# Own places for a stage's first four tiles, last rows put off, and a final norm with tokens on partitions, in a three-layer fp32 network on one core

## What is computed

```python
for i in range(2):
    h = rmsnorm(hres, norm_g[i, 0])
    m = diff_attention(h, ...) if i == 0 else short_conv(h, w_in, conv_w, w_out)
    hres = hres + rmsnorm(m, norm_g[i, 1])
    h = rmsnorm(hres, norm_g[i, 2])
    hres = hres + rmsnorm(square(relu(h @ w_up[i])) @ w_down[i], norm_g[i, 3])
x = hres[:, 16:]
# short_conv: b, c, u = split(h @ w_in); u = c * u; y = causal 3-tap conv(u); out = (b * y) @ w_out
h = rmsnorm(x, norm_gain)
z = h @ w_in                     # 25 tiles of 128 features: pool input, gates, r, k, v, decay, a
y_a = pool(...); y_b = rwkv7_time_mix(token_shift(...), ...)
x = x + concat(y_a * silu(g_a), y_b * silu(g_b)) @ w_out
out = rmsnorm(x, final_gain)
```

## Time and profile before

| | |
|---|---|
| three runs, us | 1639.82, 1643.88, 1643.98 |
| median, us | 1643.88 |
| the profiled execution: its own time / span, us | 1643.31 / 1641.5 |
| mean granted TensorE clock | 0.981 |
| TensorE products busy | 1564.2 us |
| VectorE / ScalarE / GpSimd busy | 786.0 / 619.6 / 525.7 us |

### The profile page before, as it was taken

The page is one execution under the profiler, slowest core; times in us unless marked ns, Lnnn a source line. Parts: engine busy times, 40 slices in busy tenths (PEclk is TensorE's granted clock), DMA queues, the critical chain, the costliest instruction groups (busy, mean ns, idle before and its releaser), DMA issues.

```text
span 1641.5 us, 31463 instructions
## 1 busy us (share of the span) xinstructions
PE 1564.2 (95%) x12704; PEld 1394.3 (85%) x12704; DVE 786.0 (48%) x1374; ACT 619.6 (38%) x1139; POOL 525.7 (32%) x233
## 2 busy tenths in 40 slices
PE   8999998999999999999999999999999889999895
PEld 7898978989999999989989788888889767778764
DVE  5434443754132331664436642322316798656645
ACT  5666664543132232432224532322224534433321
POOL 2222222044444444134430444444440244540020
PEclk9999999999999999999999999999999999999998
DMA  5111211132222232222222232232322122200001
GB/s 196 53 52 53 65 53 64 53 103 91 90 91 92 96 96 91 78 73 89 95 77 78 78 102 90 92 101 90 96 96 78 52 90 85 82 16 3 3 27 51
DMA packets 35691, 125.69 MB, mean 77 GB/s; under 512 B 4080, under 2 KB 4336, under 8 KB 35568
## 3 DMA queue, kind: packets, MB, share of 16 engines
q1 hardware_dynamic: 35568, 123.90, 23.5%
HBM read 121.79 MB, written 2.10 MB: 75 GB/s over the span
## 4 chain that ended last, share of the span: by engine, by line
PE 70%; DVE 11%; issue 3%; ACT 2%; DVEq 0%; ACTq 0%
PE G L1461 58%; PE ST L1782 3%; PE G L1782 3%; PE PV L1782 1%; PE PO L1782 1%; DVE wlo L922 1%; DVE rstd L883 1%; DVE m L942 1%; PE ST L1427 1%; DVE hres L949 1%; DVE acc L1351 0%; DVE t L1201 0%; DVE z L1204 0%; PE PO L1461 0%; DVE z L1193 0%
## 5 line engine op out<-in xcount | busy, mean ns | idle before, releaser
L465 POOL TENSOR_TENSOR wlo<-raw,whi 128x1024 fp32r<-128x1024 f32 x207 | 502.5, 2428 | 1073.1 <-ACT whi L517 636.7
L1461 PE MATMUL G<-xh,whi 128*128 128x258 f32 (+3 forms) x1504 | 369.6, 308 | 15.9 <-DVE t L1028 5.4
L1461 PE MATMUL G<-xl,whi 128*128 128x258 f32 (+3 forms) x1504 | 359.7, 302 | 0.0
L1461 PE MATMUL G<-xh,wlo 128*128 128x258 f32 (+3 forms) x1504 | 357.8, 300 | 1.1 <-DVE xl L890 1.1
L1461 PE MATMUL G<-ah,whi 128*128 128x256 f32 (+2 forms) x1024 | 279.6, 314 | 4.7 <-DVE al L1176 2.9
L1461 PEld LDWEIGHTS G<-xh,whi 128*128 128x128 f32 x1504 | 244.4, 190 | 39.7 <-issue 17.3
L1461 PE MATMUL G<-ah,wlo 128*128 128x256 f32 (+2 forms) x1024 | 277.8, 312 | 0.0
L1461 PE MATMUL G<-al,whi 128*128 128x256 f32 (+2 forms) x1024 | 277.7, 312 | 0.0
L527 ACT ACTIVATE whi<-raw 128x1024 fp32r<-128x1024 f32 x112 | 118.8, 1060 | 415.5 <-PE G L1461 407.4
L1461 PEld LDWEIGHTS G<-xh,wlo 128*128 128x128 f32 x1504 | 245.8, 190 | 11.0 <-DVE xl L890 1.4
L1461 PEld LDWEIGHTS G<-xl,whi 128*128 128x128 f32 x1504 | 245.1, 190 | 9.9
(11 more groups left out here) (322 smaller groups left out, 1991.3 us busy)
## 6 DMA issues: line engine op xcount, KB each, us to landing
raw<-weights_dram SPq DMA_DIRECT2D x225, 512.0 KB, 3.5
hres<-xT_dram SPq DMA_DIRECT2D x8, 264.0 KB, 5.1
out_dram<-hres SPq DMA_DIRECT2D x8, 256.0 KB, 2.1
con<-consts_dram SPq DMA_DIRECT2D x1, 512.0 KB, 7.2
mat<-mats_dram SPq DMA_DIRECT2D x1, 512.0 KB, 8.0
con<-consts_dram SPq DMA_DIRECT2D x1, 264.0 KB, 6.6
vec<-vecs_dram SPq DMA_DIRECT2D x1, 171.0 KB, 6.4
con<-consts_dram SPq DMA_DIRECT2D x1, 128.0 KB, 4.0
```

Of the source, the lines that this page charges most:

```text
L465: nc.gpsimd.tensor_tensor(wlo[:, s], raw[:, s % 2], whi[:, s].bitcast(F32), ALU.subtract)\
L1461: last_of[0] = nc.tensor.matmul(to[:, p0:p1], wt[:, w, ws], xt[:, k, t0 - off:t1_ - off], start=k == 0 and q == 0, stop=k == KT - 1 and q ...
```

## The change

**Own places, four tiles in a row.** In the first MLP chunk tiles 0 to 3 are taken out in a row, tiles 2 and 3 into the two `sq` buffers, before any low part. ScalarE reads them there. In the convolution tiles 0 to 3 are taken out before row 0 is worked on; rows use in turn `cb` and a set made of `t1` and `sq`. In the input stage tiles 0 to 3 are taken out first, and later tiles use banks 0 to 3 in turn, so that a tile waits for the fourth tile before it and not for the second.

**Late rows put off.** In the convolution's output product tile 0 and tile 1 take steps 0 to 6, then both take step 7. In the last output product seven rows are open instead of six: the seven parts of row 6 come before the parts with k = 7.

**Last norm.** TensorE multiplies chunks of 128 tokens of the squares with one column of ones, so that sums have tokens on partitions, 128x4. Root and reciprocal are of 128x4. Eight products of the broadcast reciprocal with the identity, four for each of banks 1 and 2, spread it over partitions again. VectorE scales rows 0, 1, 2, 3, 6, 7 with bank 1 as operand. ScalarE has scaled rows 4 and 5 by their gain ahead of time, copies bank 2 to `t1`, and GpSimd multiplies rows 4 and 5. Rows are stored in the order 0, 1, 2, 4, 3, 6, 5, 7.

```diff
-O2_TILES = [(o, k) for o in range(OPEN) for k in range(KT - 1)] + [(o, KT - 1) for o in range(OPEN)]
-O2_TILES += [(o, k) for o in range(OPEN, KT) for k in range(KT)]
+O2_TILES = [(o, k) for o in range(OPEN + 1) for k in range(KT - 1)] + [(o, KT - 1) for o in range(OPEN + 1)]
+O2_TILES += [(KT - 1, k) for k in range(KT)]
...
+BESIDE, ALONE = (4, 5), (0, 1, 2, 3, 6, 7)
+LAST_ORDER = (0, 1, 2, 4, 3, 6, 5, 7)
...
+        def squared_tile(c, j, s4):
+
+            return sq[:, s4 % 2] if c == 0 and j in (2, 3) else t1[:, s4 % 2]
...
+            pool.wait_ge(S("rstd_copied"), len(BESIDE) + 1)
+            for k in BESIDE:
+                nc.gpsimd.tensor_tensor(hres[:, k, META:], hres[:, k, META:], t1[:, 0, 0:SEQ], ALU.mult)\
+                    .then_inc(S("beside_ready"), 1)
...
-            stat_root(9, OUT)
+                if j - 1 in BESIDE:
+                    nc.scalar.activation(hres[:, j - 1, META:], hres[:, j - 1, META:], ACT.Copy, scale=col(V_FG, j - 1))\
+                        .then_inc(S("rstd_copied"), 1)
+            act.wait_ge(post_sum, 9)
+            nc.scalar.activation(rms[:, 0:4], G[0][:, 0:4], ACT.Sqrt, scale=1.0 / D, bias=eps_t[:, 0:1]).then_inc(rms_ready, 1)
+            act.wait_ge(S("rstd_spread"), 2)
+            nc.scalar.activation(t1[:, 0, 0:SEQ], G[1][:, 0:BANK], ACT.Copy).then_inc(S("rstd_copied"), 1)
...
-                            if n0 or c or not isinstance(j, int) or j >= 2:
+                            if c or j >= 4:
                                 dve.wait_ge(sqr_ready, j + (n0 - 1))
...
                         if c == 0:
                             for j in range(8):
-                                if j != 1:
-                                    evict(b0 + UP[c] + j, j, (b0 + UP[c] + j) % 4)
                                 if j == 0:
-                                    evict(b0 + UP[c] + 1, 1, (b0 + UP[c] + 1) % 4)
-                                low(j, (b0 + UP[c] + j) % 4)
+                                    for n in range(HELD):
+                                        evict(b0 + UP[c] + n, n, n)
+                                elif j >= HELD:
+                                    evict(b0 + UP[c] + j, j, j % 4)
+                                low(j, j % 4)
...
+            def conv_tiles(j):
+
+                return [cb[:, r] for r in range(3)] if j % 2 == 0 else [t1[:, 0, 0:NW], t1[:, 1, 0:NW], sq[:, 0, 0:NW]]
...
+            for n in range(HELD):
+                conv_tile(n)
             for j in range(KT):
...
+                for n in range(max(HELD, 3 * j), 3 * j + 3):
+                    conv_tile(n)
...
+            for j in range(HELD):
+                input_tile(j)
+            for j in range(25):
+                b = B_IN2 + j
+                if j >= HELD:
+                    input_tile(j)
...
-            stat_recip(9, OUT)
-            dve.wait_ge(rstd_ready, stat_count(9))
-            for k in range(KT):
-                nc.vector.scalar_tensor_tensor(hres[:, k, META:], hres[:, k, META:], col(V_FG, k), rstd[:, 1, META:], ALU.mult,
+            dve.wait_ge(rms_ready, stat_count(9))
+            nc.vector.reciprocal(rstd[:, 1, 0:4], rms[:, 0:4]).then_inc(rstd_ready, 1)
+            dve.wait_ge(S("rstd_spread"), 1)
+            for k in ALONE:
+                nc.vector.scalar_tensor_tensor(hres[:, k, META:], hres[:, k, META:], col(V_FG, k), G[0][:, BANK:], ALU.mult,
                                                ALU.mult).then_inc(S("out_ready"), 1)
...
-            product(B_CO, 8, a_ready, 40, ah[1], al[1], OUT, OUT[0], end=2)
+            for ks in (range(KT - 1), [KT - 1]):
+                for j in range(2):
+                    if ks[0] == 0:
+                        begin(B_CO + j)
+                    for k in ks:
+                        pe.wait_ge(a_ready, 40 + k + 1)
+                        some(G[j], j, [k], ah[1], al[1], OUT[0], block_part(OUT))
+                    if ks[0]:
+                        last_of[0].then_inc(block_done, 1)
+            product(B_CO, 8, a_ready, 40, ah[1], al[1], OUT, OUT[0], end=2, skip=2)
...
-                    product(B_IN2 + ahead, 1, x_ready, 0, x2h, x2l, OUT, 0)
+                    pe.wait_ge(lo_ready, B_IN2 + ahead + 1)
+                    pe.wait_ge(tile_out, B_IN2 + ahead - 3)
+                    some(bank(ahead % 4), ahead % 4, range(KT), x2h, x2l, META, [(*OUT, 0, SEQ)])
+                    last_of[0].then_inc(block_done, 1)
...
-            post_stat(9, OUT)
+            pe.wait_ge(psq_added, POST_ADD * 4 + half_added(KT - 2, None))
+            for t in range(4):
+                mm(G[0][:, t:t + 1], acc[:, P * t:P * t + P], ones[:, 0:1], t == 0, False)
+            pe.wait_ge(psq_ready, POST_SQ * 4 + half_square(KT - 1, None))
+            for t in range(4):
+                last = mm(G[0][:, t:t + 1], sq[:, 1, P * t:P * t + P], ones[:, 0:1], False, t == 3)
+            last.then_inc(post_sum, 1)
+            pe.wait_ge(rstd_ready, stat_count(9))
+            for b in (1, 2):
+                for t in range(4):
+                    last = mm(bank(b)[:, P * t:P * t + P], rstd[:, 1, t:t + 1].to_broadcast([P, P]), ident)
+                last.then_inc(S("rstd_spread"), 1)
```

More of the change, by code:

```diff
@@ L452, in _ @@
             blocks(sp, 0, NBLK, load)
-            for k in range(KT):
-                sp.wait_ge(S("out_ready"), k + 1)
+            for k in LAST_ORDER:
+                if k in BESIDE:
+                    sp.wait_ge(S("beside_ready"), BESIDE.index(k) + 1)
+                else:
+                    sp.wait_ge(S("out_ready"), ALONE.index(k) + 1)
                 sp.dma_start(out[k * P:(k + 1) * P, :], hres[:, k, META:]).then_inc(stored, 16)
@@ L629, in up @@
                             act.wait_ge(tile_out, b + 1)
-                            nc.scalar.activation(tile(ah[f % 2], j, slice(0, w)), t1[:, s4 % 2, 0:w], ACT.Square)\
+                            nc.scalar.activation(tile(ah[f % 2], j, slice(0, w)), squared_tile(c, j, s4)[:, 0:w], ACT.Square)\
                                 .then_inc(a_hi, 1)
                             act.wait_ge(a_ready, j + (8 * f - 1))
-                            nc.scalar.activation(act2[:, s4 % 2, 0:w], t1[:, s4 % 2, 0:w], ACT.Square)\
+                            nc.scalar.activation(act2[:, s4 % 2, 0:w], squared_tile(c, j, s4)[:, 0:w], ACT.Square)\
                                 .then_inc(sqr_ready, 1)
-                        step(b0 + UP[c], 8, up)
+                        if c == 0:
+                            for j in range(8):
+                                split(b0 + UP[c] + j + HELD, j % 4)
+                                up(b0 + UP[c] + j, j, j % 4)
+                        else:
+                            step(b0 + UP[c], 8, up)
                     if c >= 1 and c < FF_CHUNKS:
@@ L1000, in held_tile @@
                     return [(bank(g)[:, p0:p0 + o1 - o0], slice(o0, o1)) for g, p0, o0, o1 in held(cols, n, None)]
+                if b >= B_IN2:
+                    return [(bank(n % 4), slice(0, SEQ))]
                 return [(G[b % 2][:, block_slice(cols)], slice(0, cols[1] - cols[0]))]
@@ L1027, in evict @@
                             for ps, o in pieces:
-                                last = nc.vector.scalar_tensor_tensor(t1[:, s4 % 2, o], ps, 0.0,
+                                last = nc.vector.scalar_tensor_tensor(squared_tile(c, j, s4)[:, o], ps, 0.0,
                                                                       rstd[:, s % 2, cols[0] + o.start:cols[0] + o.stop],
@@ L1148, in _ @@
             last_tiles(1, B_MLP[0] + DOWN[3], NEED, B_MLP[0] + DOWN[2], (0, 3), (1, 0))
-            for j in range(KT):
-                for r in range(3):
-                    b = B_CI + 3 * j + r
-                    dve.wait_ge(block_done, b + 1)
-                    if j >= 1 and r == 0:
-                        dve.wait_ge(conv_step, 5 * j)
-                    for ps, o in held_tile(3 * j + r, b, NEED):
-                        last = nc.vector.scalar_tensor_tensor(cb[:, r, o], ps, 1.0,
-                                                              rstd[:, 0, NEED[0] + o.start:NEED[0] + o.stop],
-                                                              ALU.mult, ALU.mult)
-                    last.then_inc(tile_out, 1)
+            def conv_tiles(j):
+                return [cb[:, r] for r in range(3)] if j % 2 == 0 else [t1[:, 0, 0:NW], t1[:, 1, 0:NW], sq[:, 0, 0:NW]]
@@ new lines, in conv_tile @@
+            def conv_tile(n):
+                j, r = divmod(n, 3)
+                b = B_CI + n
+                dve.wait_ge(block_done, b + 1)
+                if j >= 2 and r == 0:
+                    dve.wait_ge(conv_step, 5 * (j - 1))
+                for ps, o in held_tile(n, b, NEED):
+                    last = nc.vector.scalar_tensor_tensor(conv_tiles(j)[r][:, o], ps, 1.0,
+                                                          rstd[:, 0, NEED[0] + o.start:NEED[0] + o.stop],
```

(4 more changed lines are left out.)

12 lines of the change are left out of this document (6 added, 6 removed).

## The result

| | before | after |
|---|---|---|
| runs on the same chip, median (least to most), us | 1643.74 (1639.82 to 1643.98), 4 runs | 1615.33 (1614.98 to 1616.69), 4 runs |
| ratio of the two, with its 95% interval | | 0.9834 (0.9817 to 0.9851) |
| profiled execution: own time / span, us | 1643.31 / 1641.5 | 1615.63 / 1613.8 |
| mean granted TensorE clock | 0.981 | 0.990 |

The kernel became 28.4 us faster. The forecast was 1611.5 in 1604 to 1620, so the sign and the range hold, and of the 32.1 us of the sum 28.4 came. The page's first part shows what kind of gain it is: TensorE's busy time fell by 9.2 us against the earlier trace rows, with 24 passes more (those of the new norm), because fewer of them ran at half clock; the other 18.5 us of the shorter span (27.7 in all) are idle time that is gone.

What follows compares the result with a forecast made beforehand. TensorE's products are busy for 95% of the span, so time can come only from its stops, with slow clock behind. Savings 3.4 + 3.3 + 6.2 + 5.7 + 4.0 + 6.2 + 3.3 = 32.1 us from 1643.31; forecast 1611.5, range 1604 to 1620.

Steps and rivals of the forecast that it cites:

- The rests: MLPs' first chunks: idle time of about 0.9 us (layer 0) and 1.1 us (layer 1) left at tile 6.
- Rival 3: First tiles of MLPs and convolution: tile 5 waits for weights, not PSUM; 12.9 us less gain, 1624; chance 0.08.
- The input stage: Input stage: both tile stops go, scan 4.4 us earlier, about 7 us stop at the key norm; 4.0 us saved.
- Rival 4: Input stage: clock stays at half behind the roughly 7 us key norm stop, making the kernel slower, to 1715; chance 0.02.
- rival 2: Input stage: freed altogether, VectorE meeting GpSimd four times less before pair 0's last BK; 8 us more, 1603; chance 0.10.
- The rule that I weighed there: Input stage: VectorE with two SBUF inputs and GpSimd reading SBUF exclude each other; two meetings more would cost 4.0 us.
- The clock: Behind seven TensorE stops: clock losses of 1.7 to 3.1 us each, counted beside the idle time.
- rival 1: MLPs, input stage, convolution: stops shrink but the clock falls all the same; 3, 4 and 1.5 us less, 1620; chance 0.15.
- The last norm: Tail behind the last product: 3.6 - 1.2 + 1.35 - 0.5 = 3.3 us saved, bounds 1.0 to 5.0.
- Spreading to bank 1 ... together 1.2 lost: Last norm: the new spread to bank 1 takes 1.05 us and handovers 0.15.
- With one store waiting behind another I add 0.5: Last norm, final stores: 0.5 us lost, added to GpSimd's rows ending 4.3 us behind the first spread against VectorE's 4.0.

## Why the prediction was right, and where not

**Stops.** Every stop that the steps removed is gone, and each comes back at its old length when its step alone is undone: 2.59 and 2.77 as 2.55 and 2.56, 3.25 as 3.27, 2.93, 4.88 and 5.06 as 4.88 and 5.07, 3.08. The rests are near the forecast: about 0.9 and 1.1 at tile 6 of the MLPs, measured 0.76 and 0.82. Rival 3 (weights are the wait) falls: none of the removed stops has left a wait for GpSimd behind. Only tile 4 waits for it, 0.88 us in the input stage and 0.87 in the second MLP (0.86 before).

**The input stage** went by its working. The scan came 22.8 - 17.6 = 5.2 us earlier (4.4 forecast), one stop of 6.81 us stood at the key norm (about 7), and behind it the clock took 0.34 x 7.42 = 2.5 (2.5 charged); the gain was 4.2 (4.0). The step's other half, the four removals ahead of the token shifts, turned out to be without effect. Rival 4 falls: the clock was back at 1.00 in the window from 1317.50 to 1330.00. So does rival 2: VectorE's chain from the scan to the last `BK` was 27.7 us long (1279.01 to 1306.68), after 28.3. The rule that I weighed there (Trainium skill, SBUF — State Buffer, Who interferes with whom) holds on both sides. Up to the last `BK` of pair 0 the token shift's second instruction met a GpSimd row twice, as it had before, and took 2.74 and 2.78 us there (2.71 and 2.78 before), 0.75 without; so the change brought no meeting more, and the 4.0 us that I weighed against it did not come. In the last norm VectorE has one operand in PSUM, and its rows took 0.74 us each (0.67 from start to start), the two that ran beside GpSimd's like the four ahead of them, as the page says of an instruction with at most one input in SBUF.

**The clock.** I gave each removed stop the slow stretch that stood behind it in one trace. In total that was right, as before to after shows, and rival 1 (the clock falls all the same) had no case behind the stops of 0.76 to 1.3 us in the changed stages. A stop need not be much longer for it, though: behind one of 1.63 us at the recurrence's start, which stands in all fourteen traces, seven have a slow stretch and seven have none. And the price is not the stop's own. With one step undone it came out (first MLP, convolution, its output, input stage, last output) as 1.6, 3.1, 1.8, 5.8 and 1.7 us where the trace of before had 1.7, 2.9, 2.9, 4.3 and 3.1, and as 0 behind the second MLP's stop, where it had 1.7. The idle time can be counted on, the clock's share can't. The undone steps' sums of 4.9 + 6.1 + 4.4 + 5.6 + 4.8 are 25.8 us; the same steps gave 28.6 from before to after, against 28.8 in the forecast. That agreement to 0.2 us is in part luck: I took the clock's prices from the very trace that the result is compared with. The Trainium skill (TensorE: Matmul & The Clock Gate, Part 1) says of the slow start of a kernel that it varies from run to run with the moment at which the work begins; the undone steps show the like in the middle of a kernel, with the same stop of 2.93 us costing 2.9 in one trace and 1.8 in another.

**The last norm** is the step that failed: 0.5 us and not 3.3. Its terms, from the tail's rows:
- root and reciprocal saved 3.6, as forecast (4.11 us from root to first row before, 0.53 to the spread now).
- "Spreading to bank 1 ... together 1.2 lost" was 2.1: at half clock its passes cost twice the price in the earlier trace rows. I had put the 16 one-column passes ahead of it at "0" and asked only for their duration, not for what clock they leave behind. The kernel with 128 columns shows this: clock at 1, and the whole spread of 16 passes in 2.05.
- VectorE's and GpSimd's rows: forecast 4.3 us behind the first spread, measured 4.86, since the second spread ran at half clock too; with the clock up it is 4.07 (1602.77 to 1606.84, the kernel with 128 columns).
- "With one store waiting behind another I add 0.5": the end came 3.9 us behind the last row and not 2.5, so 1.4.

3.6 - 2.1 + 0.5 - 1.4 and 0.1 for a later root are the 0.5 measured. That the store order makes the 1.4 was not tried by itself; one spread without GpSimd has 2.55 there.

One small slip stands in the sum as well: 1611.2 and the 0.6 by which the median lies above are 1611.8, not 1611.5.

**What was not forecast** at all is D to E, the recurrence, which no step touches: 130.95 before, 131.64 after, and between 130.1 and 131.7 in the others. It goes with where slow stretches fall: 130.1 to 130.2 in the three traces that have none in it, 131.3 to 131.7 in the seven that have one behind the stop of 1.63 us at its start.

## What to carry to other kernels

Where TensorE is nearly always busy, look for its stops in the timeline, ask the windows view for the granted clock behind each, and count the idle time as sure and the clock's share as a chance. A product that stands in TensorE's queue ahead of work that is ready stops that work too: moving three small products one tile back took 7.25 us from the input stage, more than any one step of the change gave. Where the clock has a part in a difference, read several traces of the same code: one tail here took 14.2 to 15.6 us. In a short serial end, price each new instruction at the clock that its forerunners leave behind, and check a helper engine's gain against its own preparation and the order of the stores.

## What the runs showed that I had not expected

- The granted clock fell at 1601.70 of the changed kernel's trace, in the midst of 16 passes of one column that lay back to back; with 128 columns the sums took 1.2 and 1.1 us and the clock stayed at 1 to the end of the spread.
- Of two stops of equal length in one trace (2.55 and 2.56 us, the MLPs undone), one was followed by 1.6 us of clock loss (0.22 x 7.33), the other by none. Even a stop of 1.63 us, the same in all fourteen traces, was followed by a stretch at half clock in seven of them.
- The kernel before had medians of 1643.74, 1641.64, 1639.2 and 1640.03 us in four comparisons; a change of 2 us can only be read as a ratio or in a trace.
